# Moving operands of TensorE's matmuls placed 16 to 256 bytes past the 512-byte grid of SBUF

## The chip, the cores and the metric

One Trainium2 chip (trn2), of which the kernel uses one core. The metric is the device time of one execution in microseconds (us), median over the runs shown; lower is better. A profile is one further execution, recorded by the hardware profiler.

## The reference

The computation is two transformer-like blocks in a row on one sequence of 512 tokens with 1024 features, all in float32:

```python
# first block
x = x + 0.5 * swiglu(rms_norm(x), ffn1_w_in, ffn1_w_out)           # 1024 -> 2 x 2816 -> 1024
x = x + hybrid_mixer(rms_norm(x), ...)                             # SSD scan and differential attention
x = x + memory_cross_attention(rms_norm(x), rms_norm(mem), ...)    # 256 memory rows
x = x + 0.5 * swiglu(rms_norm(x), ffn2_w_in, ffn2_w_out)
x = rms_norm(x)
# second block
q, k, v, cb, cc, cu, ga, gc = split(rms_norm(x) @ w_in)
mixed = (gate_attn * (stick_breaking(q, k, v) @ w_attn_out) + gate_conv * (conv(...) @ w_conv_out)) @ w_o
x = x + rms_norm(mixed)
x = x + rms_norm(square(relu(rms_norm(x) @ w_up)) @ w_down)        # 1024 -> 4096 -> 1024
x = x + sigmoid(rms_norm(x) @ w_ple_gate) * (p @ w_ple_proj)
```

Nearly all of the arithmetic is in products of the 512-token activations with weight matrices.

## The kernel before

**Layout.** Activations lie transposed: 128 features on the partitions, 512 tokens along the free dimension, so a chunk of an activation is 128 x 512 in float32, 2048 bytes in each partition. `gx_hi` and `gx_lo` (8 chunks each, L163 and L164) hold the normalised input of the stage that runs; `ff_hi`/`ff_lo` (22 chunks, L217 and L218) the activations inside the two FFNs; `up_hi`/`up_lo` (16 chunks, L367 and L368) those of the second block's MLP, which runs in two halves; `ys`, `o`, `ox`, `cv`, `o2`, `p` and `m` are the inputs of the smaller stages. `m_hi` and `m_lo` (the normalised memory, 8 chunks of 128 x 256, L318 and L319) are placed at 24.0625 and 32.0625 KB of the region, 64 bytes past a multiple of 512.

**Split products.** Every weight matrix comes from HBM as a stream of units of 128 x 1024 (eight blocks of 128 x 128, 512 bytes per partition each). SyncE loads a unit into a ring of four slots (L446 to L450), ScalarE rounds it to `w_hi` (L1283), GpSimd forms `w_lo = w_raw - w_hi` in four pieces (`split_unit`, L459 to L465). Activations are split the same way. Each block product is three matmuls (`products`, L512 to L518): `w_hi` with the high part, `w_hi` with the low part, `w_lo` with the high part. In these the weight block is the stationary operand and the activation chunk the moving one. Each matmul has a weight load of its own (PEld in the profile).

**Where the activation is the stationary operand.** `token_group` (L662 to L684) computes outputs with tokens on the partitions, for the stages z, v and v2 and for the memory's values (cv): here a 128 x 128 piece of the activation is loaded into the array, and the weights `w_hi`, `w_lo` are moving, 512 wide (L678 to L680).

**Halves.** In the stages o2 and down_b, and in the stages that start behind them, a chunk is worked in two halves of 256 tokens (`split_tail`, `group_by_halves`), so those matmuls have 128 x 256 moving.

**Order.** The order of the work on each engine is written out by hand; engines meet at semaphores alone. TensorE waits for a unit's `w_lo` (`unit_lo`), for the chunk of the activation (`gx_lo_done` and the like) and for a free PSUM bank (`tile_free`). A ring slot is loaded again once `w_lo` of its unit is made; ScalarE and GpSimd overwrite `w_hi` and `w_lo` once TensorE is done with the unit.

**Addresses.** `fixed` (L152) hands out addresses in steps of 64 bytes from the base of SBUF upward; `x`, `cols` and the weights of dt (`wdt`, `wdt_hi`) come first, then the cursor is rounded up to 2048 (L161) and `gx_hi`, `gx_lo`, `w_raw`, `w_hi`, `w_lo` follow, all on the 2048 grid. `wdt_hi` begins 448 bytes past a multiple of 512 and has eight blocks of 64 bytes, so its blocks begin at eight different places of the grid; L785 to L787 use them as stationary operands of 128 x 16. The rest of the tiles share a region that begins at a multiple of 512 (`REGION`, L181), at offsets given in KB (`at`). Buffers of the attention (`prob`, `w_T`, `o_nrm` and others, `in_gx`, L266) lie in the space of `gx_hi`/`gx_lo` while these are not used. The lowest 16384 bytes of each partition are reserved as scratch for DMA descriptors, by default.

Of the kernel before, what the change touches and what calls it, by code (L numbers as in the profile page):

```python
# [18 lines left out]
F32R = mybir.dt.float32r  # L19
# [3 lines left out]
ds = bass.ds  # L23

P = 128
S = 512
TT = S // P
D = 1024
DC = D // P
FF = 2816  # L30
FC = FF // P
# [4 lines left out]
LINE = 2048  # L36
# [10 lines left out]
HC = FF2 // P // 2  # L47
# [52 lines left out]
def build(nc, wstream, xT, memT, pT, cols_d, rows_d, wdt_d, relb_d, consts_d, onehot_d, pen_d, out):  # L100
    ctx = ExitStack()
    with ctx:
        sems = {}

        def sem(name):
            if name not in sems:
                sems[name] = ctx.enter_context(nc.semaphore(name))
            return sems[name]
# [36 lines left out]
        def ffn_count(name, k):  # L145

            return (FC if name == "ffn2" else 0) + k


        cursor = [(nc.sbuf_base + 63) // 64 * 64]  # L150

        def fixed(name, shape, dt=F32):  # L152
            t = nc.alloc_sbuf_tensor_at(name, [P] + shape, dt, offset=cursor[0])
            cursor[0] += (int(np.prod(shape)) * 4 + 63) // 64 * 64
            return t
# [2 lines left out]
        cols = fixed("cols", [NCOLS])  # L158
        wdt = fixed("wdt", [8, 16])
        wdt_hi = fixed("wdt_hi", [8, 16], F32R)  # L160
        cursor[0] = -(-cursor[0] // LINE) * LINE  # L161
        GX_HI, GX_LO = cursor[0], cursor[0] + DC * S * 4
        gx_hi = fixed("gx_hi", [DC, S], F32R)  # L163
        gx_lo = fixed("gx_lo", [DC, S], F32R)  # L164
        w_raw = fixed("w_raw", [RING, UNIT])
        w_hi = fixed("w_hi", [RING, UNIT], F32R)
        w_lo = fixed("w_lo", [RING, UNIT], F32R)
# [10 lines left out]
        xsum = fixed("xsum", [16])  # L178
        xrec = fixed("xrec", [16])
        y_sq, y_root, y_rstd = xmin, xsum, xrec  # L180
        REGION = -(-cursor[0] // 512) * 512  # L181
        cursor[0] = REGION + 96 * 1024 + 64
        rstd_col = fixed("rstd_col", [TT])
        root_col = fixed("root_col", [2 * TT])
        eps_col = fixed("eps_col", [1])
# [6 lines left out]
        def at(name, kb, shape, dt=F32):  # L192
            off = REGION + int(kb * 1024)
            size = int(np.prod(shape)) * 4
            assert off + size <= REGION_END, (name, off + size - REGION_END)
            return nc.alloc_sbuf_tensor_at(name, [P] + shape, dt, offset=off)
# [3 lines left out]
        def first(i):  # L200
            return isinstance(i, int) and i == 0

        def tile_of(buf, c):

            if isinstance(c, int):
                return buf[:, c, :]
            n = buf.shape[2]
            return buf[:, :, :].rearrange("p a b -> p (a b)")[:, ds(c * n, n)]

        def col(name, i):  # L210
            return cols[:, COLS[name] + i:COLS[name] + i + 1]
# [2 lines left out]
            return cols[:, ds(COLS[name] + i, 1)]  # L214


        ff_hi = at("ff_hi", 0, [FC, S], F32R)  # L217
        ff_lo = at("ff_lo", 44, [FC, S], F32R)  # L218
        ff_gate = at("ff_gate", 88, [S])
        ff_silu = at("ff_silu", 90, [S])  # L220
        ff_up = at("ff_up", 92, [S])
        ff_act = at("ff_act", 94, [S])
        sumsq2 = at("sumsq2", 88, [S])
        square2 = at("square2", 90, [S])

        z_tok = at("z_tok", 0, [TT, D])
        bc = at("bc", 16, [8, S])
# [136 lines left out]
            return early_sq[:, idx, :] if name == "pmlp" and idx < 4 else post_sq[:, m, tok(a)]  # L364

        post_sum = rfin_row
        up_hi = at("up_hi", 16, [HC, S], F32R)  # L367
        up_lo = at("up_lo", 48, [HC, S], F32R)  # L368
        f_acc = at("f_acc", 80, [DC, S])
        up_t = at("up_t", 0, [S])  # L370
        up_a = at("up_a", 2, [S])
        p_T = at("p_T", 4, [2, S])
# [20 lines left out]
        def wait(eng, s, value):  # L393

            if not isinstance(value, int) or value > 0:
                eng.wait_ge(s, value)

        def blocks(eng, n, body, peel=0):

            for i in range(peel):  # L400
                body(i)
            if n - peel == 1:
                body(n - 1)
            elif n > peel:
                with eng.Fori(peel, n) as i:
                    body(i)
# [104 lines left out]
        def _(pe):  # L511
            def products(slot, blk, dst, rhs, first, last):  # L512

                hi = w_hi[:, slot, blk * P:(blk + 1) * P]
                lo = w_lo[:, slot, blk * P:(blk + 1) * P]
                nc.tensor.matmul(dst, hi, rhs[0], start=first, stop=False)  # L516
                nc.tensor.matmul(dst, hi, rhs[1], start=False, stop=False)  # L517
                return nc.tensor.matmul(dst, lo, rhs[0], start=False, stop=last)  # L518

            def tiles(stage, rhs, chunks, body, peel=0, ready=None, n=S, hooks=(), banks=2, together=1, count=0, before=2, opening=None):  # L520

                per = -(-chunks // UC)
                assert (body * per) % RING == 0
                at_block = dict(hooks)

                def block_of(i):  # L530
                    start = 0
                    if first(i) and together > 1:
                        start = together
                        wait(pe, tile_free, TILE0[stage] - 1)
                        if opening:
                            opening()
                        for k in range(chunks if not opening else 0):
                            ready(k)
                            for j in (0, 2, 1) if k == 0 else range(together):
                                if k == 0:  # L540
                                    pe.wait_ge(unit_lo, UNIT0[stage] + j + 1)
                                if k == 0 and j == 1:
                                    pe.wait_ge(tile_free, TILE0[stage])
                                mm = products((UNIT0[stage] + j) % RING, k, bank[j][:, 0:n], rhs(k), k == 0,
                                              k == chunks - 1)
                                if k == chunks - 1:
                                    mm.then_inc(unit_done, 1)
                        if (together - 1, chunks - 1) in at_block:
                            at_block[(together - 1, chunks - 1)]()
                    for j in range(start, body):  # L550
                        T = TILE0[stage] + i * body + j
                        free = T - banks + 1
                        if first(i) and j < min(before, banks):
                            free = max(free, T - before + 1) if before <= banks else T - before + 1
                        wait(pe, tile_free, free)
                        dst = bank[j % banks][:, 0:n]
                        for uu in range(per):
                            jj = j * per + uu
                            pe.wait_ge(unit_lo, UNIT0[stage] + i * (body * per) + (jj + 1))
                            kk = range(uu * UC, min(chunks, (uu + 1) * UC))  # L560
                            for k in kk:
                                if ready and (first(i) and j == 0):
                                    ready(k)
                                mm = products((UNIT0[stage] + jj) % RING, k - uu * UC, dst, rhs(k),
                                              k == 0, k == chunks - 1)
                                if first(i) and (j, k) in at_block:
                                    at_block[(j, k)]()
                            mm.then_inc(unit_done, 1)
                blocks(pe, (count or TILES[stage]) // body, block_of, peel)
# [149 lines left out]
            def gx_ready(name):  # L719
                return lambda k: pe.wait_ge(sem("gx_lo_done"), gx_count(name, k + 1))  # L720
# [48 lines left out]
            def ffn(name, norm, before, hooks=(), opening=None):  # L769
                tiles(f"{name}_in", gx, DC, 4, peel=1, ready=gx_ready(before),  # L770
                      hooks=norm_hooks(norm, before, together=3) + hooks, banks=4, together=3, opening=opening)

                def act_ready(k):
                    if k % UC == 0:
                        pe.wait_ge(sem("ffn_act_lo"), ffn_count(name, min(FC, k + UC)))
                tiles(f"{name}_out", lambda k: (ff_hi[:, k, :], ff_lo[:, k, :]), FC, 4, peel=1, ready=act_ready)


            ffn("ffn1", "n_ffn1", "load", hooks=(((3, 7), brow_sums),), opening=opening_group)
# [233 lines left out]
            for j in range(3, 8):  # L1013
                for k in range(DC):
# [4 lines left out]
                  ready=lambda k: pe.wait_ge(sem("m_lo"), k + 1), hooks=(((0, 5), m_rows),), before=5)  # L1019
# [244 lines left out]
        def _(act):  # L1264
# [37 lines left out]
            def next_operand(stage, weight, i, j, m, T, src, src_ready):  # L1302

                act.wait_ge(src_ready, T)
                nc.scalar.activation(tile_of(gx_hi, m), tile_of(src, m), ACT.Copy, scale=col_at(weight, m))\
                  .then_inc(sem("gx_hi_done"), 1)
                act.wait_ge(sem("summed"), sum_count(stage, m + 1))
                nc.scalar.activation(square[:, :], tile_of(src, m), ACT.Square).then_inc(sem("squared"), 1)
# [1307 lines left out]
```

## Time and profile before

| | |
|---|---|
| median of 2 runs | 2135.09 us (2134.69 to 2135.49) |
| profiled execution, span from first to last instruction | 2133.4 us |
| TensorE busy | 2114.8 us, 10122 matmuls |
| weight loads | 1740.7 us |
| VectorE, ScalarE, GpSimd busy | 829.8, 803.6, 1120.5 us |
| HBM read | 204.31 MB, 98 GB/s |

The profiled execution's own time is its span of 2133.4 us; what a run takes outside the span is not in the profile. A matmul's duration in the profile includes the time in which it overlaps the next one, so what a stream of matmuls costs is read from the distance between their starts in the timeline, not from their durations. "PE" is the matmul side of TensorE and "PEld" its weight loads. In the profile an entry `bank<-gx_hi,w_hi` names the moving operand first and the stationary one second.

### The profile page before, as it was taken

What the parts mean: (1) busy time and instruction counts of PE and PEld (TensorE: products, weight loads), DVE (VectorE), ACT (ScalarE), POOL (GpSimd) and SP (SyncE); (2) the same over time, 40 slices, a digit from 0 to 9 for tenths busy, and PEclk for the clock granted to TensorE, in tenths of its full rate; (3) what the DMA queues carried; (4) which work ended last, traced back from release to release, by engine and by line L of the source; (5) the groups of instructions that cost most, each with busy time, mean ns of one, the idle gap of its engine ahead of it and who ended that gap; (6) DMA issues with size and microseconds to landing.
All of it is one profiled execution on the core that took longest, in us unless ns stands there. A gap on an engine that the chain in (4) does not pass through costs nothing.

```text
span 2133.4 us, 29164 instructions
## 1 busy us (share of the span) xinstructions
PE 2114.8 (99%) x10122; PEld 1740.7 (82%) x10122; DVE 829.8 (39%) x1489; ACT 803.6 (38%) x1345; POOL 1120.5 (53%) x1493
## 2 busy tenths in 40 slices
PE   9999999999999999999999999999999999999999
PEld 7888888878887778877888888887787888888887
DVE  5222211762841766143322222208744474023244
ACT  5222232325834655323322223326554343122233
POOL 6555555673354337725655555554545466555554
PEclk9999999999999999999999999999999999999999
DMA  6322233233322213412332223321222223332322
GB/s 214 119 98 98 99 106 106 85 99 96 114 99 79 75 55 122 155 40 89 99 98 98 95 94 117 99 96 63 79 89 79 89 80 108 99 99 99 99 89 80
DMA packets 61344, 207.71 MB, mean 97 GB/s; under 512 B 6616, under 2 KB 8088, under 8 KB 61256
## 3 DMA queue, kind: packets, MB, share of 16 engines
q1 hardware_dynamic: 55216, 195.84, 27.8%
q10 hardware_dynamic: 6040, 10.65, 1.5%
q8 instruction: 61, 1.00, 0.2%
q14 instruction: 27, 0.22, 0.0%
HBM read 204.31 MB, written 4.77 MB: 98 GB/s over the span
## 4 chain that ended last, share of the span: by engine, by line
PE 42%; issue 28%; POOL 27%; DVE 2%; POOLq 0%; ACT 0%; DMA 0%; SPq 0%; DVEq 0%; ACTq 0%
POOL w_lo L463 27%; PE bank L516 11%; PE bank L518 11%; PE bank L517 11%; PE bank L678 1%; PE bank L680 1%; PE bank L679 1%; PE bank L908 1%; PE bank L932 1%; PE bank L840 1%; PE bank L920 0%; DVE gx_lo L2394 0%; DVE bank L2403 0%; PE bank L846 0%; DVE x L2405 0%
## 5 line engine op out<-in xcount | busy, mean ns | idle before, releaser
L463 POOL TENSOR_TENSOR w_lo<-w_raw,w_hi 128x256 fp32r<-128x256 f32 x1448 | 1087.1, 783 | 933.4 <-ACT w_hi L1283 933.3
L516 PE MATMUL bank<-gx_hi,w_hi 128*128 128x512 f32 (+1 forms) x1768 | 674.9, 382 | 7.8 <-DVE gx_lo L2394 4.5
L518 PE MATMUL bank<-gx_hi,w_lo 128*128 128x512 f32 (+1 forms) x1768 | 668.1, 378 | 0.0
L517 PE MATMUL bank<-gx_lo,w_hi 128*128 128x512 f32 (+1 forms) x1768 | 667.6, 378 | 0.0
L1283 ACT CAST w_hi<-w_raw 128x1024 fp32r<-128x1024 f32 x364 | 378.4, 1045 | 347.9 <-PE bank L518 291.8
L516 PEld LDWEIGHTS bank<-gx_hi,w_hi 128*128 128x128 f32 x1768 | 332.6, 188 | 74.2 <-DVE gx_lo L2394 6.4
L518 PEld LDWEIGHTS bank<-gx_hi,w_lo 128*128 128x128 f32 x1768 | 332.5, 188 | 62.1
L517 PEld LDWEIGHTS bank<-gx_lo,w_hi 128*128 128x128 f32 x1768 | 332.7, 188 | 60.5 <-issue 0.2
L516 PE MATMUL bank<-ff_hi,w_hi 128*128 128x512 f32 x352 | 136.9, 389 | 0.0
L517 PE MATMUL bank<-ff_lo,w_hi 128*128 128x512 f32 x352 | 136.9, 389 | 0.0
L518 PE MATMUL bank<-ff_hi,w_lo 128*128 128x512 f32 x352 | 136.9, 389 | 0.0
L516 PE MATMUL bank<-up_hi,w_hi 128*128 128x512 f32 (+1 forms) x288 | 105.4, 366 | 0.0
L517 PE MATMUL bank<-up_lo,w_hi 128*128 128x512 f32 (+1 forms) x288 | 105.3, 365 | 0.0
L518 PE MATMUL bank<-up_hi,w_lo 128*128 128x512 f32 (+1 forms) x288 | 105.3, 365 | 0.0
L1854 DVE TENSOR_TENSOR ff_up<-bank,rstd_row 128x512 f32<-128x512 f32 x44 | 30.4, 690 | 189.9 <-PE bank L518 189.9
L1355 ACT CAST ff_hi<-ff_act 128x512 f32 (+1 forms) x44 | 27.3, 620 | 188.8 <-DVE ff_act L1858 188.8
L518 PEld LDWEIGHTS bank<-ff_hi,w_lo 128*128 128x128 f32 x352 | 66.1, 188 | 13.8
L516 PEld LDWEIGHTS bank<-ff_hi,w_hi 128*128 128x128 f32 x352 | 66.1, 188 | 13.7
L517 PEld LDWEIGHTS bank<-ff_lo,w_hi 128*128 128x128 f32 x352 | 66.1, 188 | 13.6
L1351 ACT ACTIVATE ff_silu<-ff_gate 128x512 f32<-128x512 f32 x44 | 27.8, 632 | 119.7 <-DVE ff_gate L1851 119.7
L1851 DVE TENSOR_TENSOR ff_gate<-bank,rstd_row 128x512 f32<-128x512 f32 x44 | 30.4, 691 | 90.7 <-PE bank L518 90.6
L678 PE MATMUL bank<-w_hi,gx_hi 128*128 128x512 f32 x160 | 63.7, 398 | 0.4 <-ACT z_tok L1337 0.4
(358 smaller groups left out, 2703.4 us busy)
## 6 DMA issues: line engine op xcount, KB each, us to landing
w_raw<-wstream SPq DMA_DIRECT2D x364, 512.0 KB, 3.5
bias_spread<-bias_rows ACTq DMA_DIRECT2D x1, 2560.0 KB
square<-cum_rows ACTq DMA_DIRECT2D x8, 256.0 KB, 3.5
rfin_row<-cum_rows ACTq DMA_DIRECT2D x8, 256.0 KB, 3.1
outT<-ple_o SPq DMA_DIRECT2D x8, 256.0 KB, 2.0
x<-xT SPq DMA_DIRECT2D x3, 512.0 KB, 8.0
square<-bias_spread ACTq DMA_DIRECT2D x4, 256.0 KB, 2.6
rfin_row<-bias_spread ACTq DMA_DIRECT2D x4, 256.0 KB, 2.7
```

Source lines behind the costliest of these rows:

```text
L463: ins = nc.gpsimd.tensor_tensor(w_lo[:, s, part], w_raw[:, s, part], w_hi[:, s, part].bitcast(F32), ALU.subtract)
L516: nc.tensor.matmul(dst, hi, rhs[0], start=first, stop=False)
L517: nc.tensor.matmul(dst, hi, rhs[1], start=False, stop=False)
L518: return nc.tensor.matmul(dst, lo, rhs[0], start=False, stop=last)
L678: nc.tensor.matmul(dst, a[0], rh, start=(k == 0), stop=False, skip_group_check=True)
L679: nc.tensor.matmul(dst, a[1], rh, start=False, stop=False, skip_group_check=True)
L680: mm = nc.tensor.matmul(dst, a[0], rl, start=False, stop=(k == DC - 1), skip_group_check=True)
L1283: nc.scalar.copy(w_hi[:, j, :], w_raw[:, j, :]).then_inc(unit_hi, 1)
L1351: nc.scalar.activation(ff_silu[:, :], ff_gate[:, :], ACT.Silu).then_inc(sem("ffn_silu"), 1)
L1355: nc.scalar.copy(tile_of(ff_hi, c), ff_act[:, :]).then_inc(sem("ffn_act_hi"), 1)
L1851: nc.vector.tensor_tensor(ff_gate[:, :], bank[2 * j][:, :], rstd_row[:, :], ALU.mult)\
L1854: nc.vector.tensor_tensor(ff_up[:, :], bank[2 * j + 1][:, :], rstd_row[:, :], ALU.mult)\
```

## The change

Only addresses and row lengths change; no instruction is added or removed.

- `gx_hi` and `gx_lo` begin 64 bytes past the 2048 grid. The cursor is rounded up again behind them, so `w_raw`, `w_hi`, `w_lo` stay on it.
- The rows of `ff_hi` and `ff_lo` are 16 and 64 bytes longer than a chunk (S + 4 and S + 16 elements): chunk k begins 16 k and 64 k bytes further along the grid. `tile_of` and the caller cut a chunk back to 512 elements.
- `up_hi` and `up_lo` begin 128 and 256 bytes past the grid.
- The shared region is 4 KB longer and begins on the 2048 grid; some tiles of it move by multiples of 512 bytes. The room comes from the scratch for DMA descriptors, 1024 bytes per partition in place of 16384.

```diff
-        cursor[0] = -(-cursor[0] // LINE) * LINE
+        cursor[0] = -(-cursor[0] // LINE) * LINE + 64
         GX_HI, GX_LO = cursor[0], cursor[0] + DC * S * 4
         gx_hi = fixed("gx_hi", [DC, S], F32R)
         gx_lo = fixed("gx_lo", [DC, S], F32R)
+        cursor[0] = -(-cursor[0] // LINE) * LINE
         w_raw = fixed("w_raw", [RING, UNIT])
...
-        REGION = -(-cursor[0] // 512) * 512
-        cursor[0] = REGION + 96 * 1024 + 64
+        REGION = -(-cursor[0] // LINE) * LINE
+        cursor[0] = REGION + 100 * 1024 + 64
...
             if isinstance(c, int):
-                return buf[:, c, :]
+                return buf[:, c, 0:min(S, buf.shape[2])]
             n = buf.shape[2]
-            return buf[:, :, :].rearrange("p a b -> p (a b)")[:, ds(c * n, n)]
+            return buf[:, :, :].rearrange("p a b -> p (a b)")[:, ds(c * n, min(n, S))]
...
-        ff_hi = at("ff_hi", 0, [FC, S], F32R)
-        ff_lo = at("ff_lo", 44, [FC, S], F32R)
-        ff_gate = at("ff_gate", 88, [S])
...
+        ff_hi = at("ff_hi", 0, [FC, S + 4], F32R)
+        ff_lo = at("ff_lo", 45, [FC, S + 16], F32R)
+        ff_gate = at("ff_gate", 92, [S])
...
-        up_hi = at("up_hi", 16, [HC, S], F32R)
-        up_lo = at("up_lo", 48, [HC, S], F32R)
-        f_acc = at("f_acc", 80, [DC, S])
+        up_hi = at("up_hi", 16.125, [HC, S], F32R)
+        up_lo = at("up_lo", 48.25, [HC, S], F32R)
+        f_acc = at("f_acc", 80.5, [DC, S])
...
-                tiles(f"{name}_out", lambda k: (ff_hi[:, k, :], ff_lo[:, k, :]), FC, 4, peel=1, ready=act_ready)
+                tiles(f"{name}_out", lambda k: (ff_hi[:, k, 0:S], ff_lo[:, k, 0:S]), FC, 4, peel=1, ready=act_ready)
...
-    nc = bacc.Bacc("TRN2", target_bir_lowering=False, num_devices=1)
+    nc = bacc.Bacc("TRN2", target_bir_lowering=False, num_devices=1, dynamic_dma_scratch_size=1024)
```

## Rows read from the trace of the kernel before

**Rows 1.** The page: the span, and part 1 (engine, busy us, share).

```profile
span 2133.4 us, 29164 instructions
PE 2114.8 (99%) x10122; PEld 1740.7 (82%) x10122; DVE 829.8 (39%) x1489; ACT 803.6 (38%) x1345; POOL 1120.5 (53%) x1493
...
PEclk9999999999999999999999999999999999999999
```

**Rows 2.** Waits of PE: who waited for whom, total us, times, longest us.

```profile
PE bank L516 <- DVE gx_lo L2394: 4.5, 9, 0.9
PE bank L516 <- POOL w_lo L463: 2.3, 3, 1.1
```

**Rows 3.** Groups by form: line engine op, out<-in, count | busy, mean ns | idle before.

```profile
L463 POOL TENSOR_TENSOR w_lo<-w_raw,w_hi 128x256 fp32r<-128x256 f32 x1448 | 1087.1, 783 | 933.4 <-ACT w_hi L1283 933.3
L1283 ACT CAST w_hi<-w_raw 128x1024 fp32r<-128x1024 f32 x364 | 378.4, 1045 | 347.9 <-PE bank L518 291.8 <-PE bank L680 42.8 <-DMA w_raw<-wstream 8.8
```

**Rows 4.** Groups by form: the matmuls whose operands the change moves.

```profile
L516 PE MATMUL bank<-gx_hi,w_hi 128*128 128x512 f32 x1576 | 618.9, 393 | 1.4 <-DVE cc_t L2262 0.6 <-DVE q_T L1995 0.6
L516 PE MATMUL bank<-gx_hi,w_hi 128*128 128x256 f32 x192 | 56.0, 292 | 6.4 <-DVE gx_lo L2394 4.5 <-POOL w_lo L463 2.0
L734 PE MATMUL bank<-gx_hi,w_hi 128*128 128x512 f32 x24 | 9.8, 409 | 1.5 <-DVE gx_lo L1805 1.5
L516 PE MATMUL bank<-ff_hi,w_hi 128*128 128x512 f32 x352 | 136.9, 389 | 0.0
L516 PE MATMUL bank<-up_hi,w_hi 128*128 128x512 f32 x224 | 87.1, 389 | 0.0
L516 PE MATMUL bank<-up_hi,w_hi 128*128 128x256 f32 x64 | 18.3, 285 | 0.0
L678 PE MATMUL bank<-w_hi,gx_hi 128*128 128x512 f32 x160 | 63.7, 398 | 0.4 <-ACT z_tok L1337 0.4
L932 PE MATMUL bank<-v_tok,w_T 128*128 128x128 f32 x160 | 19.1, 275 | 0.0
```

**Rows 5.** Timeline of PE, moving ff, 512 wide, both operands on the grid.

```profile
299.81 0.39 PE L516 MATMUL bank<-ff_hi,w_hi 128*128 128x512 f32 x1
...
305.93 0.39 PE L516 MATMUL bank<-ff_hi,w_hi 128*128 128x512 f32 x1
```

**Rows 6.** Timeline of PE, moving gx, 256 wide, both operands on the grid.

```profile
1684.76 0.28 PE L517 MATMUL bank<-gx_lo,w_hi 128*128 128x256 f32 x1
...
1697.47 0.28 PE L518 MATMUL bank<-gx_hi,w_lo 128*128 128x256 f32 x1
```

**Rows 7.** Timeline of PE, moving m, 256 wide, 64 bytes past the grid.

```profile
841.83 0.28 PE L516 MATMUL bank<-m_hi,w_hi 128*128 128x256 f32 x1
...
855.37 0.28 PE L517 MATMUL bank<-m_lo,w_hi 128*128 128x256 f32 x1
```

**Rows 8.** Timeline of PE, weights moving, gx stationary, both on the grid.

```profile
465.64 0.39 PE L680 MATMUL bank<-w_lo,gx_hi 128*128 128x512 f32 x1
...
470.40 0.39 PE L680 MATMUL bank<-w_lo,gx_hi 128*128 128x512 f32 x1
```

**Rows 9.** Timeline of PE, weights moving, m stationary, 64 bytes past the grid.

```profile
860.04 0.39 PE L679 MATMUL bank<-w_hi,m_lo 128*128 128x512 f32 x1
...
863.54 0.40 PE L679 MATMUL bank<-w_hi,m_lo 128*128 128x512 f32 x1
```

**Rows 10.** Timeline of PE, moving gx, wdt stationary in 64-byte blocks.

```profile
459.62 0.40 PE L785 MATMUL bank<-gx_hi,wdt_hi 128*16 128x512 f32 x1
...
464.95 0.40 PE L787 MATMUL bank<-gx_hi,wdt_lo 128*16 128x512 f32 x1
```

**Rows 11.** Timeline of PE, float32 operands, 512 wide, eight merged.

```profile
920.58 3.60 PE L1081 MATMUL bank<-pxT,vx 128*128 128x512 f32 x8
```

**Rows 12.** Instructions on vx: count, duration ns min/median/max.

```profile
L1081 PE MATMUL bank<-pxT,vx x32: 590/592/595, 920.6 to 962.4; 128*128 128x512 f32 x32
```

**Rows 13.** The page, part 3: DMA queue, kind: packets, MB, share of 16 engines.

```profile
q1 hardware_dynamic: 55216, 195.84, 27.8%
q10 hardware_dynamic: 6040, 10.65, 1.5%
```

More of the change, by code:

```diff
@@ L214, in col_at @@
             return cols[:, ds(COLS[name] + i, 1)]
-        ff_hi = at("ff_hi", 0, [FC, S], F32R)
-        ff_lo = at("ff_lo", 44, [FC, S], F32R)
-        ff_gate = at("ff_gate", 88, [S])
[L220 to L224, printed above, removed]
+        ff_hi = at("ff_hi", 0, [FC, S + 4], F32R)
+        ff_lo = at("ff_lo", 45, [FC, S + 16], F32R)
+        ff_gate = at("ff_gate", 92, [S])
+        ff_silu = at("ff_silu", 94, [S])
+        ff_up = at("ff_up", 96, [S])
+        ff_act = at("ff_act", 98, [S])
+        sumsq2 = at("sumsq2", 92, [S])
+        square2 = at("square2", 94, [S])
         z_tok = at("z_tok", 0, [TT, D])
```

## The prediction

> **What bounds the kernel now.** I read the page first. TensorE's matmul side is busy 99% of the span, at the full granted clock (2.4 GHz) in all forty slices; no other engine is over 53% [rows 1]. Then the waits: the longest waits of TensorE for anyone sum to 4.5 and 2.3 us of a span of 2133.4 [rows 2]. The chain of waits goes through GpSimd's `w_lo` for 27% of the span, but that is a chain of buffers and not a bound: GpSimd idles 933 us before L463, always for ScalarE's `w_hi`, and ScalarE idles 348 us before L1283, nearly all of it for TensorE to finish a unit [rows 3]. One unit costs GpSimd four pieces of 783 ns, 3.1 us, and TensorE 24 matmuls of 226.7 ns (below), 5.4 us. So the kernel's time is the number of matmuls times the distance between their starts, and a change of that distance comes through one to one, in either direction, in nearly every stage.
>
> Durations of matmuls overlap, so I take distances from the timeline. With both operands on the 512 grid and 512 columns, 27 steps take 6.12 us: 226.7 ns each [rows 5]. The columns alone are 512 / 2.4 = 213.3 ns, so 13.3 ns come on top. With 256 columns it is 12.71 us for 106 steps, 119.9 ns, again 13.3 over the 106.7 of the columns [rows 6]. These 13.3 ns are all that an address can give back; they are 6% of the matmul. Weights on the moving side and the input on the stationary side, on the grid, show the same: 4.76 us for 21 steps, 226.7 ns [rows 8].
>
> **What the trace already shows of operands off the grid.** The kernel holds three such places, and they decide the sum.
> - The memory's `m_hi`/`m_lo` are moving operands that begin 64 bytes past the grid, as `gx` will: 13.54 us for 115 steps, 117.7 ns [rows 7], 2.2 ns less than on the grid at the same width.
> - The same tiles as stationary operands, with weights moving 512 wide: 3.50 us for 15 steps, 233.3 ns [rows 9], 6.6 ns more than `gx` on the grid in the same code [rows 8].
> - `wdt` is a stationary operand whose eight blocks begin at eight different places of the grid, with `gx` moving 512 wide: 5.33 us for 23 steps, 231.7 ns [rows 10], 5.0 ns more.
>
> So the place matters, but by a few ns, and with both signs. The Trainium skill (TensorE: Matmul & The Clock Gate, the weight-load step in part 2) says that the moving and the stationary operand have independent read ports and that loading the next weights takes no read bandwidth from the running matmul; by that the change would leave the time as it is. The differences among rows 6 to 10 speak against taking it literally.
>
> **The counts** [rows 4]; each row stands for one of three matmuls of a product. Moving `gx`, 512 wide: 1576 and 24 times three, with 24 of `wdt`, 4824. Moving `gx`, 256 wide: 192 x 3 = 576. Moving `ff`: 352 x 3 = 1056. Moving `up`: 224 x 3 = 672 at 512 wide, 64 x 3 = 192 at 256 wide. Together 6552 at 512 and 768 at 256 columns, 7320 of the 10122 matmuls. Stationary `gx` in z, v and v2: 160 x 3 = 480.
>
> **The terms.**
> 1. `gx` moving at 64 bytes, 256 wide: this is the case of rows 7. 576 x -2.2 ns = -1.3 us.
> 2. `gx` moving at 64 bytes, 512 wide: not in the trace. Ends: -10.0 ns, all of the 13.3 except what a matmul of plain float32 shows (eight of L1081 in 3.60 us with 592 ns for the last [rows 11, 12]: 430 ns apart, 3.3 over the 426.7 of twice 512 columns); and +6.6 ns as in rows 9. I take the row that is nearest in kind, same offset on the same side: -2.2 ns x 4824 = -10.6 us (ends -48 and +32).
> 3. `gx` as the stationary operand 64 bytes off: the diff says that the input moves and that the weights stay, but in z, v and v2 the input is what is loaded. This is the case of rows 9: 480 x +6.6 = +3.2 us.
> 4. `ff`: with rows 16 and 64 bytes longer the 22 chunks walk through the grid. Nearest are the walking blocks of rows 10: 1056 x +5.0 = +5.3 us (ends -10.0 and +6.6 each: -10.6 and +7.0 us).
> 5. `up` at 128 and 256 bytes: fixed offsets, none of which any row has. Ends again -10.0 and +6.6 ns on 864, -8.6 and +5.7 us; between the -2.2 of rows 7 and the +5.0 of rows 10 I take nothing.
> 6. `w_T`, `prob` and `o_nrm` in the space of `gx` become stationary operands 64 bytes off: 160 of L932 [rows 4] and fewer of the other two, under 300 in all, plain float32 and 128 wide. Between -6.6 and +6.6 ns each, at most 2 us; I take nothing.
> 7. ScalarE, VectorE and GpSimd write and read the moved tiles with the same instructions. They have 53% or less of the span; a few ns on any is covered by TensorE's stream. What would be uncovered are the hand-overs of rows 2, 6.8 us in all, and no row gives a reason for them to move. The descriptor scratch is only shrunk; nearly all transfers of the page go through two hardware queues [rows 13] that load from HBM while TensorE never waits for a DMA, so nothing is taken for it, gain or loss.
>
> Sum: -1.3 - 10.6 + 3.2 + 5.3 = -3.4 us. Against the profiled execution that is 2133.4 - 3.4 = 2130.0 us; the median of the runs shown lies 1.7 us over the profiled span, so the forecast for the metric is 2131.7, said as 2132 us.
>
> **Where a gain would go.** If the matmuls shorten, nothing else is late soon: at 216.7 ns a unit takes TensorE 5.2 us against GpSimd's 3.1. Only the short hand-overs of the halves (L2394 behind L516) would grow a little.
>
> **The rivals.**
> - *The extra time is all a meeting of the two reads, and an odd start takes it away.* Every moving operand then loses 10.0 ns: 7320 x 10.0 = 73 us, less the 3.2 of term 3: 2065 us, faster by 3.3%. For it: plain float32 matmuls [rows 11, 12] show that a stream with weight loads can run with 3.3 ns over its columns, and the 13.3 are the same at 256 and 512 columns, as a meeting within the 128 columns of a weight load would be. Against: at 64 bytes, the very offset chosen for `gx`, rows 7 show 2.2 given back and not 10. The Trainium skill (same page, Back-to-back issue gap) gives 512 / 2.4 + 2.5 = 215.8 ns for an isolated warm matmul of 512 columns; the trace has 226.7 on the grid, and by the page's figure this rival would end at about 2058 us. Over 2% needs 6.3 ns of each of the 7320.
> - *The grid is the good case at 512 columns.* Both rows with 512 columns and an operand off the grid are slower (rows 9 and 10), and the faster one has 256. If all 6552 of 512 columns go the way of rows 9, it is 6552 x 6.6 = +43.2, -1.7 for the 768 narrow ones, +3.2 for term 3: +44.7, 2180 us, slower by 2.1%. The place is the stream of L516 to L518 in every large stage, the price 5.0 to 6.6 ns a matmul; with 5.0 (rows 10) it ends at 2169 us. Against: in both rows it is the stationary operand that is off. It passes 2% from 6.3 ns on.
> - *The moving operand's start makes no difference.* Only the stationary `gx` pays, 2135.1 + 3.2 = 2138 us. Against it stand rows 6 and 7. This is what the Trainium skill's rule of the two read ports (TensorE: Matmul & The Clock Gate, part 2) would give in this kernel.
> - *The change does not do what it says.* The chunk of `gx` is 2048 bytes and a half is 1024, so all of them begin 64 off; `REGION` is on the 2048 grid, so 128 and 256 hold for `up`. Only its second half, that weights stay on one side and inputs on the other, is untrue, and that is term 3.
>
> **How the numbers follow.** Mixed small effects as in the sum, 2115 to 2150 us: 0.50. No effect of the moving side, 2138 us, which lies within that: 0.13 more. Grid best at 512 columns: 0.20, of which 0.07 over 2%. A gain of more than the sum's: 0.17, of which 0.10 over 2%. About 2% is what a measurement of this kernel can tell from no change. So faster by over 2% (under 2092): 0.10; within: 0.83; slower (over 2178): 0.07. The range leaves out about 0.11 below and 0.09 above: 2096 to 2168 us.
>
> **What would show it.** In the profile after: distances of 224.5 ns in the stream of L516 to L518 with `gx` moving and 512 wide (step 2), near 118 at 256 wide (step 1), 233 at L678 to L680 (step 3), about 231 and uneven in the stages of `ff` (step 4), 220 to 233 with `up` (step 5). PE would stay at 99% busy, and its waits as in rows 2. The forecast is wrong if `gx` at 512 columns runs at 217 ns or at 231 to 233; that one term carries two thirds of all matmuls moved.

## The result, and the profile after

| | before | after |
|---|---|---|
| median | 2135.09 us | 2153.78 us (2153.11 to 2154.46, 2 runs) |
| ratio | | 1.0086, 95% interval 1.0062 to 1.0110 |
| span of the profiled execution | 2133.4 us | 2151.3 us |

The changed kernel is slower by 18.7 us, 0.9%. That is inside the forecast range, but on the other side of it: 3.4 us of gain were forecast. The page of the changed kernel (span, part 1, and the granted clock of part 2) shows that what became longer is TensorE's own stream:

```profile
span 2151.3 us, 29164 instructions
PE 2133.7 (99%) x10122; PEld 1741.7 (81%) x10122; DVE 828.4 (39%) x1489; ACT 803.5 (37%) x1345; POOL 1123.6 (52%) x1493
...
PEclk9999999999999999999999999999999999999999
```

The instructions are the same in number, the other engines are within 4 us of [rows 1], and PE's busy time rose by 18.9 us. The granted clock is 2.4 GHz but for one stretch that a digit of 54 us cannot show. Behind two waits of TensorE, 1.09 us for `w_lo` and 0.90 us for `gx_lo`, it is at 1.2 GHz for 3.4 us, with 18 matmuls in that time (a row of `--windows`: the stretch and its length, busy us and count of PE, PEld, DVE, ACT and POOL, the granted share of the clock, the DMA share and GB/s):

```profile
1729.13:1732.54 3.41, 3.41 (x18) 3.41 (x18) 1.94 (x5) 1.08 (x3) 3.12 (x6) 0.50 0.23 60
```

The profiled execution of the kernel before has no such stretch between 5 and 2131 us. Such stretches come without the edit too: of the kernel before, as it was timed beside the experiments, the executions with a mean clock of 0.998 or 0.999 took on average 1.5 and 0.8 us longer than those with 1.000 (4 against 15, and 4 against 17 executions). Both timed executions of the changed kernel had a mean clock under 1, so about 1 us of the 18.7 is the clock's and some 17 to 18 us are the edit's.

The waits of PE in the changed kernel (lines are one further down than before) are no longer than those of [rows 2]:

```profile
PE bank L517 <- DVE gx_lo L2395: 3.4, 7, 0.9
PE bank L517 <- POOL w_lo L464: 2.3, 3, 1.1
```

So the distances have to be read. Timelines of PE in the changed kernel, each time the first and the last matmul of an undisturbed stretch (start us, us, engine, line, operation); first `gx` moving, 512 wide, 64 bytes past the grid, 45 steps, then the same 256 wide, 48 steps:

```profile
79.74 0.39 PE L518 MATMUL bank<-gx_lo,w_hi 128*128 128x512 f32 x1
...
90.04 0.39 PE L518 MATMUL bank<-gx_lo,w_hi 128*128 128x512 f32 x1
...
1700.74 0.28 PE L519 MATMUL bank<-gx_hi,w_lo 128*128 128x256 f32 x1
...
1706.39 0.28 PE L519 MATMUL bank<-gx_hi,w_lo 128*128 128x256 f32 x1
```

10.30 us / 45 = 228.9 ns where [rows 5] had 226.7; 5.65 / 48 = 117.7 ns where [rows 6] had 119.9. The same tile at the same address is 2.2 ns slower than on the grid at 512 columns and 2.2 ns faster at 256. Next, `gx` stationary in stage z (23 steps), the walking rows of `ff` (61 steps), and `up` (45 steps):

```profile
470.63 0.39 PE L679 MATMUL bank<-w_hi,gx_hi 128*128 128x512 f32 x1
...
475.99 0.40 PE L681 MATMUL bank<-w_lo,gx_hi 128*128 128x512 f32 x1
...
285.78 0.39 PE L517 MATMUL bank<-ff_hi,w_hi 128*128 128x512 f32 x1
...
299.86 0.39 PE L518 MATMUL bank<-ff_lo,w_hi 128*128 128x512 f32 x1
...
1857.68 0.39 PE L518 MATMUL bank<-up_lo,w_hi 128*128 128x512 f32 x1
...
1867.98 0.39 PE L518 MATMUL bank<-up_lo,w_hi 128*128 128x512 f32 x1
```

These are 233.0 ns for the stationary `gx` (226.7 in [rows 8], 233.3 for `m` in [rows 9]), 230.8 ns for `ff` and 228.9 ns for `up`.

### The profile page after: what moved, and what is told of

It is laid out like the page before. It is cut to its first block, busy times and chain, and to the rows that moved or that the text cites. A ratio compares the mean times of both kernels' runs of the same rounds, so it can differ in the third digit from the quotient of the medians.

```text
span 2151.3 us, 29164 instructions
## 1 busy us (share of the span) xinstructions
PE 2133.7 (99%) x10122; PEld 1741.7 (81%) x10122; DVE 828.4 (39%) x1489; ACT 803.5 (37%) x1345; POOL 1123.6 (52%) x1493
## 4 chain that ended last, share of the span: by engine, by line
PE 42%; issue 28%; POOL 27%; DVE 2%; ACT 0%; POOLq 0%; DMA 0%; DVEq 0%; ACTq 0%
POOL w_lo L464 27%; PE bank L517 11%; PE bank L519 11%; PE bank L518 10%; PE bank L679 1%; PE bank L681 1%; PE bank L680 1%; PE bank L909 1%; PE bank L933 1%; PE bank L841 1%; PE bank L921 0%; DVE gx_lo L2395 0%; DVE bank L2404 0%; DVE x L2406 0%; PE bank L847 0%
## 5 line engine op out<-in xcount | busy, mean ns | idle before, releaser
L517 PE MATMUL bank<-gx_hi,w_hi 128*128 128x512 f32 (+1 forms) x1768 | 681.5, 385 | 7.0 <-DVE gx_lo L2395 3.4
L519 PE MATMUL bank<-gx_hi,w_lo 128*128 128x512 f32 (+1 forms) x1768 | 671.5, 380 | 0.0
L518 PE MATMUL bank<-gx_lo,w_hi 128*128 128x512 f32 (+1 forms) x1768 | 667.8, 378 | 0.0
L517 PEld LDWEIGHTS bank<-gx_hi,w_hi 128*128 128x128 f32 x1768 | 332.9, 188 | 72.6 <-DVE gx_lo L2395 5.3
L519 PEld LDWEIGHTS bank<-gx_hi,w_lo 128*128 128x128 f32 x1768 | 332.4, 188 | 68.6
L518 PEld LDWEIGHTS bank<-gx_lo,w_hi 128*128 128x128 f32 x1768 | 332.7, 188 | 63.6 <-issue 0.2
L518 PE MATMUL bank<-ff_lo,w_hi 128*128 128x512 f32 x352 | 138.5, 393 | 0.0
L519 PE MATMUL bank<-ff_hi,w_lo 128*128 128x512 f32 x352 | 138.4, 393 | 0.0
L517 PE MATMUL bank<-ff_hi,w_hi 128*128 128x512 f32 x352 | 138.0, 392 | 0.0
L517 PE MATMUL bank<-up_hi,w_hi 128*128 128x512 f32 (+1 forms) x288 | 106.4, 369 | 0.0
L519 PE MATMUL bank<-up_hi,w_lo 128*128 128x512 f32 (+1 forms) x288 | 105.7, 367 | 0.0
L518 PE MATMUL bank<-up_lo,w_hi 128*128 128x512 f32 (+1 forms) x288 | 104.9, 364 | 0.0
L517 PEld LDWEIGHTS bank<-ff_hi,w_hi 128*128 128x128 f32 x352 | 66.1, 188 | 15.3
L518 PEld LDWEIGHTS bank<-ff_lo,w_hi 128*128 128x128 f32 x352 | 66.0, 188 | 15.3
L519 PEld LDWEIGHTS bank<-ff_hi,w_lo 128*128 128x128 f32 x352 | 66.1, 188 | 14.9
```

## The experiments

All but the last, which is an edit of the kernel before, are variants of the changed kernel in which the starts of `gx`, `ff`, `up` and the weights are set one by one; rows of `ff` are 2048 bytes long unless said. The kernel before was timed beside them on the same chip, at 2135.1 to 2135.3 us. The distances below are taken from the timelines as above, over 43 steps or more of 512 columns in the stages of `ffn1` (`gx`, `ff`) and in the second block's MLP (`up`), if no other count is given. A start is printed to 0.01 us, so a distance taken over 43 steps can be off by 0.2 ns. The code cuts show the main lines of each edit; in all of them but the last `f_acc` also moves by 512 bytes.

**Which part costs: each alone.** `gx64`:

```diff
-        ff_hi = at("ff_hi", 0, [FC, S + 4], F32R)
-        ff_lo = at("ff_lo", 45, [FC, S + 16], F32R)
+        ff_hi = at("ff_hi", 0 / 1024, [FC, S + 0], F32R)
+        ff_lo = at("ff_lo", 45 + 0 / 1024, [FC, S + 0], F32R)
...
-        up_hi = at("up_hi", 16.125, [HC, S], F32R)
-        up_lo = at("up_lo", 48.25, [HC, S], F32R)
...
+        up_hi = at("up_hi", 16 + 0 / 1024, [HC, S], F32R)
+        up_lo = at("up_lo", 48.5 + 0 / 1024, [HC, S], F32R)
```

> Only gx_hi and gx_lo begin 64 bytes past the grid; ff and up are back on it. Theory A (the cost of a place adds up matmul by matmul): 4824 wide moving gx at 229.1 in place of 226.7 ns is +11.6 us, 576 narrow ones at 117.7 is -1.3 us, 480 stationary gx at 233.3 is +3.2 us: 2148.6 us, with ff and up at 226.7 ns. Rival B (the loss comes from something that all parts share, the moved region or the smaller descriptor scratch): gx alone gives back little of the loss, and ff and up stay above 226.7 ns.

Measured: 2146.9 us, ratio 1.0054 (1.0037 to 1.0071): +11.6 us, 1.7 less than expected. `gx` at 512 columns is at 228.6 ns over one stretch (10.06 us / 44) and at 228.9 over all long ones, `ff` and `up` are back at 226.7.

`ffwalk` has `+ 64` taken from the cursor of `gx`, and `up` as in `gx64`; the rows of `ff` stay longer.

> Only the rows of ff_hi and ff_lo are 16 and 64 bytes longer; gx and up on the grid. Theory A: 1056 matmuls at 230.8 in place of 226.7 ns, +4.4 us: 2139.5 us, all other stages as before. Rival B: over 2143 us, with gx off 226.7 ns too.

Measured: 2139.8 us, ratio 1.0021 (1.0011 to 1.0030), +4.5 us, as theory A has it.

`up_only` has `gx` and `ff` on the grid and `up` at 128 and 256 bytes.

> Only up_hi and up_lo begin 128 and 256 bytes past the grid. Theory A: 672 wide matmuls at 229.0 in place of 226.7 ns is +1.6 us, 192 narrow ones about -0.1: 2136.6 us. Rival B: over 2141 us.

Measured: 2136.7 us, ratio 1.0006 (0.9996 to 1.0015), +1.4 us: in the trace the 672 wide matmuls cost 1.5 us more; in the time alone it would not be told from nothing. The three parts sum to 17.5 us of the 18.7, and the 1.2 us left over are about what the slower clock of both executions of the changed kernel costs.

`grid` puts all three back on the grid and keeps the longer region and the small descriptor scratch.

> Every moving operand is back on the grid, but the shared region is as in the changed kernel (longer, on the 2048 grid) and the scratch for descriptors stays at 1024 bytes. Theory A (all of the loss is in the distances of the matmuls): 2135.2 us, within 0.1% of before. Rival B (region or scratch cost something): 1 us or more above it, the part of the loss that the three parts run alone leave over (18.7 - 11.6 - 4.5 - 1.4 = 1.2 us).

Measured over five rounds: 2135.35 us, ratio 1.0002 (0.9993 to 1.0011). The interval, -1.5 to +2.3 us, would still hold the 1.2 us of rival B, but the trace does not: its span is 2133.5 us against 2133.4 before, with `gx`, `ff` and `up` at 226.7 ns. So region and scratch cost nothing that is seen, and the 1.2 us have the other explanation just given.

**Is it the place of an operand, or its distance from the other?** `both64` moves the weights by the same 64 bytes as `gx`, and leaves all other activations on the grid:

```diff
         cursor[0] = -(-cursor[0] // LINE) * LINE + 64
...
         gx_lo = fixed("gx_lo", [DC, S], F32R)
-        cursor[0] = -(-cursor[0] // LINE) * LINE
+        cursor[0] = -(-cursor[0] // LINE) * LINE + 64
         w_raw = fixed("w_raw", [RING, UNIT])
         w_hi = fixed("w_hi", [RING, UNIT], F32R)
         w_lo = fixed("w_lo", [RING, UNIT], F32R)
+        cursor[0] = -(-cursor[0] // 512) * 512
         consts = fixed("consts", [7 * P])
```

> gx and the weights w_raw, w_hi, w_lo all begin 64 bytes past the grid, every other activation is on it. Theory C (only the distance between the starts of the moving and the stationary operand counts): gx stages are back at 226.7 ns, at L679 to L681 too, while ff, up and the other activations, now 64 bytes behind their weights, go to 233.3 ns: about 2544 wide matmuls at +6.6 is +16.8 us, 2152 us. Rival D (each operand that is off the grid costs by itself): moving gx has 2.4 and 6.6 ns on top of 226.7, 235.7 ns, in all +43 us there, +4 at L679 to L681 and +17 elsewhere: about 2200 us.

Measured: 2148.7 us, ratio 1.0063 (1.0046 to 1.0080). The timeline of PE in `both64`, lines two further down than in the listing: `gx` moving (45 steps), `ff` moving (43 steps), weights moving over a stationary `m` (36 steps):

```profile
79.71 0.39 PE L518 MATMUL bank<-gx_hi,w_hi 128*128 128x512 f32 x1
...
89.91 0.39 PE L518 MATMUL bank<-gx_hi,w_hi 128*128 128x512 f32 x1
...
299.81 0.39 PE L520 MATMUL bank<-ff_hi,w_lo 128*128 128x512 f32 x1
...
309.85 0.39 PE L518 MATMUL bank<-ff_hi,w_hi 128*128 128x512 f32 x1
...
861.80 0.39 PE L680 MATMUL bank<-w_hi,m_hi 128*128 128x512 f32 x1
...
869.96 0.39 PE L680 MATMUL bank<-w_hi,m_hi 128*128 128x512 f32 x1
```

`gx`, 64 bytes off together with its weights, is back at 226.7 ns. `ff`, on the grid but now 64 bytes behind its weights, runs at 233.5 without having been moved. And the stationary `m`, 64 bytes off as ever, falls from 233.3 [rows 9] to 226.7, since the weights that move over it are now 64 off too. D falls, and theory C is shown for this one common shift of 64 bytes: what counts is the distance of the moving operand's start from the stationary one's, not the place of either. The kernel as a whole is slower by 0.6%, since every other activation was left behind. The time is 3 us under what C gave, by two things in the trace. The wide matmuls lost 14.9 us and not 16.8: where other work breaks the stream, they are over 226.7 ns in the kernel before too and had less to lose. And the sum left out `up` at 256 columns, `m` moving and `m` stationary, which together became 2.0 us shorter.

**Which distances.** Three stages, each with another start, in one kernel; weights on the grid. `scan1` has `gx` at 256, `ff` at 128, `up` at 32 bytes:

```diff
-        cursor[0] = -(-cursor[0] // LINE) * LINE + 64
+        cursor[0] = -(-cursor[0] // LINE) * LINE + 256
...
+        ff_hi = at("ff_hi", 128 / 1024, [FC, S + 0], F32R)
+        ff_lo = at("ff_lo", 45 + 128 / 1024, [FC, S + 0], F32R)
...
+        up_hi = at("up_hi", 16 + 32 / 1024, [HC, S], F32R)
+        up_lo = at("up_lo", 48.5 + 32 / 1024, [HC, S], F32R)
```

> Moving operands at constant starts, weights on the grid: gx at 256, ff at 128, up at 32 bytes. Theory E (the pattern repeats every 256 bytes): gx at 226.7 ns, its stationary use too. Theory F (it repeats every 512): gx at 256 lies elsewhere, 228 to 236 ns, about the 231 that a matmul shows on average right after a restart. For 128 and 32 bytes neither has a number; 64 bytes gave 229.1, so 227 to 232 ns is expected for both, and under 224 ns would show a start that beats the grid. Time by E about 2137, by F about 2150 us.

Measured: 2146.3 us, ratio 1.0054 (1.0034 to 1.0074), not the 2137 of E, because `ff` and `up` went higher than I had allowed. The timeline of PE in `scan1` (`gx` 45 steps, `ff` 44, `up` 43):

```profile
79.63 0.39 PE L519 MATMUL bank<-gx_hi,w_lo 128*128 128x512 f32 x1
...
89.83 0.39 PE L519 MATMUL bank<-gx_hi,w_lo 128*128 128x512 f32 x1
...
299.73 0.39 PE L518 MATMUL bank<-ff_lo,w_hi 128*128 128x512 f32 x1
...
309.99 0.39 PE L517 MATMUL bank<-ff_hi,w_hi 128*128 128x512 f32 x1
...
1865.78 0.40 PE L518 MATMUL bank<-up_lo,w_hi 128*128 128x512 f32 x1
...
1875.81 0.39 PE L519 MATMUL bank<-up_hi,w_lo 128*128 128x512 f32 x1
```

At 256 bytes it is 10.20 us / 45 = 226.7 ns, exactly the grid's; at 128 and 32 bytes 233.2 and 233.3. The stationary `gx` is at 226.7 too, as E has it.

`scan2` has `gx` at 192, `ff` at 480, `up` at 384; `scan3` has `gx` at 32, `ff` at 320, `up` at 96.

> gx at 192, ff at 480 (32 before the grid), up at 384 bytes. Theory E: 192 is the same as 64 before the grid, so gx shows the 233.3 ns that an operand 64 bytes behind the weights showed, and up shows what ff shows at 128 bytes. Theory F: 192 and 384 have numbers of their own. By E gx costs 4824 x 6.6 = +32 us: about 2168 us.

> gx at 32, ff at 320, up at 96 bytes. Theory E: ff at 320 is the same as 64, 229.1 ns. Theory C (the place alone counts, not the stage): gx at 32 shows the number that up shows at 32 in the run before last. Time between 2137 and 2150 us.

Measured: `scan2` 2173.9 us, ratio 1.0177 (1.0148 to 1.0207); `scan3` 2172.9 us, 1.0173 (1.0143 to 1.0203). Theory E gave 2168 us for the first, for `gx` alone; for the second I had asked for 2150 at most, having no number for 32 bytes. Their distances are in the table below. The last experiment of this kind, `scan4`, has `gx` at 160, and `ff` and `up` 16 and 8 bytes into a slightly larger tile:

```diff
+        def shifted(name, kb, start, chunks):
+            whole = at(name, kb, [chunks * S + 8], F32R)
+            return whole[:, start // 4:start // 4 + chunks * S].rearrange("p (a b) -> p a b", b=S)
...
+        ff_hi = shifted("ff_hi", 0, 16, FC)
...
+        up_hi = shifted("up_hi", 16, 8, HC)
```

> gx at 160, ff at 16, up at 8 bytes past the grid, weights on it. The starts seen so far show 226.7 ns at 0 and 256, 229 at 64 and 320, and 232 to 233.3 at 32, 96, 128, 192, 384, 448 and 480. Theory G (0 and 256 are the best places of all): 160, 16 and 8 all show between 227 and 234 ns, and the kernel takes about 2135 + 4824 x 6.6 ns = 2167 us, plus up to 11 for ff and up. Rival H (a start within one 16-byte line of the grid, or at 160, gives back part of the 13.3 ns): one of them shows under 225 ns.

Measured: 2179.8 us, ratio 1.0209 (1.0190 to 1.0228). From the timelines of `scan4` (lines five further down than in the listing), `gx` (43 steps) and `ff` (44 steps), the `ff` line standing for a start within 16 bytes:

```profile
79.79 0.39 PE L521 MATMUL bank<-gx_hi,w_hi 128*128 128x512 f32 x1
...
89.86 0.39 PE L522 MATMUL bank<-gx_lo,w_hi 128*128 128x512 f32 x1
...
299.80 0.40 PE L523 MATMUL bank<-ff_hi,w_lo 128*128 128x512 f32 x1
...
309.99 0.40 PE L522 MATMUL bank<-ff_lo,w_hi 128*128 128x512 f32 x1
```

All distances at 512 columns together, by the moving start less the stationary one, modulo 512:

| bytes | ns | from |
|---|---|---|
| 0 | 226.7 | before, and `both64` with both at 64 |
| 8, 16 | 232.5 (233.3 in the later stage of up), 231.6 | `scan4`, up and ff |
| 32 | 233.3, 233.4 | `scan1` up, `scan3` gx |
| 64 | 228.9 | after, gx |
| 96, 128 | 233.4, 233.2 | `scan3` up, `scan1` ff |
| 160, 192 | 234.2, 233.4 | `scan4` gx, `scan2` gx |
| 256 | 226.7 | `scan1` gx |
| 320 | 228.9 | `scan3` ff |
| 384 | 232.5 | `scan2` up |
| 448, 480 | 233.5, 233.4 | `both64` ff, `scan2` ff |

The pattern repeats at 256 bytes for 0 and 256, 64 and 320, 192 and 448. It does so only roughly for 128 and 384: over all long stretches these are 233.3 and 232.4 ns, so theory E is not exact. Nor does it hang on the stage (32 bytes in `gx` and in `up`). The same kernels hold a check the other way round, with weights moving over the stationary `gx` (start of the weights less that of `gx`, modulo 256): 226.7 ns at 0 (`scan1`), 228.8 at 64 (`scan2`), 233.3 at 224 and 96 (`scan3`, `scan4`).

Of the fourteen starts none is under the grid's 226.7. H falls: no start gives back any of the 13.3 ns. Theory G holds but for small misses: 160 bytes is at 234.2, just over its 234, and the time is 2 us over its 2178.

Two things say that the distance is not the whole of it. One stretch of 48 matmuls with `gx` moving (from 1441.4 us in the changed kernel, and the same one, from 1436.5 us, in `gx64`) runs at 233.3 ns, although its distance is the 64 bytes of all the others at 228.9. And the table does not add up matmul by matmul where the starts change within a stream: `up` in the changed kernel has two matmuls at 128 bytes and one at 256 in every product, which by the table would be 231.0 ns on average, and it runs at 228.9.

**The one place that was off the grid before.** `m192` is the kernel before with the memory's tiles moved:

```diff
-        m_hi = at("m_hi", 24.0625, [DC, ML], F32R)
-        m_lo = at("m_lo", 32.0625, [DC, ML], F32R)
+        m_hi = at("m_hi", 24.1875, [DC, ML], F32R)
+        m_lo = at("m_lo", 32.1875, [DC, ML], F32R)
```

> The kernel before, with m_hi and m_lo at 192 instead of 64 bytes past the grid (and three small tiles beside them by the same 128 bytes). By the distances measured: as a moving operand 256 wide, 192 past the weights is what 64 before them is, 113.3 in place of 117.7 ns, 192 x -4.4 = -0.8 us; as the stationary operand the weights then move 64 past it (mod 256), 229.1 in place of 233.3 ns, 96 x -4.2 = -0.4 us. Together -1.2 us: 2134.0, at the edge of what five rounds tell; the trace should show both numbers. Rival: m at 192 shows 118 and 233 ns, and the time is that of before.

Measured over five rounds: 2134.7 us, ratio 0.9997 (0.9988 to 1.0006), no difference by this measure. Counting only executions with a mean clock of 1.000, the median is 2134.2 us (8 executions) against 2135.1 (17), a gain of somewhat under 1 us. The timeline of PE in `m192`, 256 columns with `m` moving (72 steps) and 512 with `m` stationary (27 steps):

```profile
841.73 0.28 PE L517 MATMUL bank<-m_lo,w_hi 128*128 128x256 f32 x1
...
849.89 0.28 PE L517 MATMUL bank<-m_lo,w_hi 128*128 128x256 f32 x1
...
857.74 0.39 PE L680 MATMUL bank<-w_lo,m_hi 128*128 128x512 f32 x1
...
863.92 0.39 PE L680 MATMUL bank<-w_lo,m_hi 128*128 128x512 f32 x1
```

8.16 us / 72 = 113.3 ns and 6.18 / 27 = 228.9 ns, against 117.7 and 233.3 [rows 7, 9]. The second number is as expected, and is worth 0.4 us. The first looks like a hit and is none: 113.3 ns does not need the 192 bytes. `grid` and `up_only` have `m` and the weights at the very same addresses, 64 bytes apart, and the same stretch runs differently in them (`grid` first, then `up_only`, 72 steps each):

```profile
839.75 0.28 PE L517 MATMUL bank<-m_hi,w_hi 128*128 128x256 f32 x1
...
848.23 0.28 PE L517 MATMUL bank<-m_hi,w_hi 128*128 128x256 f32 x1
...
840.06 0.28 PE L517 MATMUL bank<-m_hi,w_hi 128*128 128x256 f32 x1
...
848.22 0.28 PE L517 MATMUL bank<-m_hi,w_hi 128*128 128x256 f32 x1
```

That is 117.8 and 113.3 ns. `gx64` and `scan1`, with `m` at 64 bytes too, also show 113.3, and the first stretch of `m192`, 29 matmuls from 833.2 us, shows 117.8 with `m` at 192. So at 256 columns 64 and 192 bytes share two values, and a stretch takes one of them within a few matmuls of its start; what decides which is not shown. The 113.3 that the expectation was worked out from has the same flaw: `up` in `both64` runs at 113.3 in one stretch and at 117.8 in the next. `m192` shows the 0.4 us of the stationary side; whether its other half is a gain that stays is open.

## Why the prediction was wrong

The mean distances of all matmuls of a kind, times their number, in the two profiled executions (us, after less before; a distance to a later restart is included):

| step | forecast | measured |
|---|---|---|
| 1: `gx` moving, 256 wide, 576 | -1.3 | -0.6 |
| 2: `gx` moving, 512 wide, 4824 | -10.6 | +9.3 |
| 3: `gx` stationary, 480 | +3.2 | +2.6 |
| 4: `ff`, 1056 | +5.3 | +4.4 |
| 5: `up`, 864 | 0 | +1.5 |
| 6, 7: attention's tiles, everything else | 0 | +0.7 |
| sum | -3.4 | +17.9 |

**The step that failed is the second**, and with it the sign of the whole. I had two rows for a thing that the trace did not hold: the same offset on the same side, at 256 columns (-2.2 ns), and another offset on the other side, at 512 columns (+6.6 and +5.0). I took the first as "nearest in kind". What the change showed is that the width decides the sign: `gx` at 64 bytes is 2.2 ns faster at 256 columns and 2.2 ns slower at 512, in one kernel. So step 2 had -2.2 ns a matmul where +2.2 was measured in the steady stretches, -10.6 us where the trace has +9.3. The 20 us between forecast and measurement of this one term are nearly all of the 22 us of error. The step was guessed between ends of -48 and +32 us, and its weight, two thirds of all matmuls moved, was in the text; a value of 0 there would have been the honest middle, and would still have given a forecast on the slower side.

**Steps 1, 3, 4** came out in place: 117.7 ns at 256 columns, 233.0 against 233.3 ns for the stationary `gx`, 230.8 against 231.7 for the walking rows. Each had a row of the same kind in the trace of before. For step 1 that was partly luck: the row it rests on [rows 7] could as well have read 113.3, as it does in `up_only`. In us, 1 and 3 are a little smaller since not every matmul reached its steady distance before the stream was broken by other work; 12 matmuls of step 1 also fell into the stretch at 1.2 GHz. **Step 5** had no row and was taken as nothing; `up` runs at 228.9 ns, less than the 233.2 of 128 bytes alone, its two parts being at 128 and 256. **Steps 6 and 7** held: `grid` shows region and scratch at nothing that is seen, and the waits stayed as in [rows 2]. Of the +0.7 us, 0.4 are sums of squares on TensorE, four of which fell into the stretch at 1.2 GHz.

**The bound was right.** The distances always sum to the span, so that both grew by 17.9 us says nothing by itself. What bears the bound out is that 17.2 of them lie in the matmuls whose operands moved, and that no wait of TensorE grew by more than 0.2 us.

**The rivals.** That the grid is the good case at 512 columns is what happened, at 2.2 ns for `gx` in place of the 5.0 to 6.6 of its price, since 64 bytes happens, by luck, to be the mildest of the off-grid places tried; with `gx` at 192, 32 or 160 bytes (`scan2` to `scan4`, `ff` and `up` off the grid too) the full price was paid and the loss was 1.7 to 2.1%, 29 to 34 us of it in the wide matmuls with `gx` moving. The rival had 0.20 and deserved more: both rows at 512 columns pointed to it, and I argued against them that their stationary operand was the one off the grid. `both64` shows that this is no difference in kind, since their distance is what counts there; the rows 9 and 10 were rows of other distances of the same curve. The rival of the full gain, that an odd start takes away the meeting of two reads, is half right in an instructive way: the places of the two operands do act together (`both64`), but the grid is already its best place at this width. The Trainium skill's sentence on the two independent read ports (TensorE: Matmul & The Clock Gate, part 2), read as the prediction reads it, that the operands' places make no difference, does not describe what these runs show: `ff` in `both64` went from 226.7 to 233.5 ns when of its two operands the weights alone were moved. The third rival, that only the stationary `gx` pays, falls with the +9.3 us of step 2.

**What stays open.** That the reads of the moving operand and of the next weights meet somewhere is an inference from the role of their distance; no run here shows the reads themselves. Nor is it shown what the 13.3 ns at distance 0 consist of, why one distance can have two values, or why a stream needs from about five to ten matmuls to settle after a break (in the kernel before, eight of them behind the transposes of stage z, 224 to 236 ns apart).

## What to carry to other kernels

When a stream of float32r matmuls bounds the kernel, keep the moving operand and the weight tiles at the same start modulo 256 bytes if the moving side has 512 columns: every distance tried except 0 and 256 cost 1.0% to 3.3% of a matmul in this kernel. Measure the distance between starts at the width, and with the pair of operands, that the change will have; a row of another width can have the other sign. Where one operand must be moved, move its partner with it, and count first what else shares that partner: in `both64` the streams of `gx` were mended and the others paid. Before a distance is put down to an edit, look for it in runs without the edit, as the 113.3 ns of `m192` teach.

## What the runs showed of the hardware

- The distance between two float32r matmuls depends on the start of the moving operand relative to that of the stationary one: 226.7 ns at 0 and 256 bytes, 228.9 at 64 and 320 (233.3 in one stretch at 64), 231.6 to 234.2 at the other ten, for 512 columns at the full clock.
- For 256 columns at the full clock the picture is another one, and several distances have two values, each steady over a stretch. In ns, by bytes modulo 512, over all long stretches of the runs:

| bytes | ns | from |
|---|---|---|
| 0, 256 | 120.0 | before (`gx`, `up`), `both64` (`gx`, `m`), `scan1` (`gx`) |
| 8 | 120.0 or 126.7 | `scan4`, `up` |
| 32 | 117.8 or 116.7 | `scan1` `up`, `scan3` `gx` |
| 64 | 117.8 or 113.3 | before and `up_only`, `m` |
| 96 | 120.0 | `scan3`, `up` |
| 160 | 118.6 or 117.3 | `scan4`, `gx` |
| 192, 448 | 113.3 or 117.8 | `scan2` `gx` and `m192` `m`, `both64` `up` |
| 384 | 118.6 | `scan2`, `up` |

- Moving both operands by 64 bytes changes nothing: 226.7 ns at 512 columns, 120.0 at 256.
- Single distances can be uneven where the mean is steady, and differ at one and the same distance of 64 bytes. In the packed trace of the changed kernel, whose starts are whole ns, the steps with `gx` moving go through a cycle of three: 232 ns after L517, 226 after L518, 229 after L519. In the kernel before, on the grid, they are 226 or 227. The timeline's 0.01 us cannot show this.
- The granted clock can fall to 1.2 GHz for a few us within a stream: 3.4 us in the changed kernel, behind waits of 1.09 and 0.90 us, with matmuls of 256 columns 0.21 to 0.22 us apart in place of 0.12.
